# Sums of squares over feature blocks gathered on VectorE, and layer norms made in one pass, in a float32 two-block transformer kernel

## The reference

```python
def rms_norm(x, g):
    xf = x.astype(jnp.float32)
    y = xf * lax.rsqrt(jnp.mean(xf * xf, axis=-1, keepdims=True) + NORM_EPS)
    return (y * g.astype(jnp.float32)).astype(x.dtype)

def layer_norm(x, g, b):
    xf = x.astype(jnp.float32)
    mu = jnp.mean(xf, axis=-1, keepdims=True)
    var = jnp.mean(jnp.square(xf - mu), axis=-1, keepdims=True)
    return ((xf - mu) * lax.rsqrt(var + LN_EPS) * g + b).astype(x.dtype)

# first block
h = rms_norm(x, g_mix)                      # norm 1
...                                         # projections, sparse attention, conv, memory attention, gates
x = x + merged @ w_o
h = rms_norm(x, g_ffn)                      # norm 2
x = x + (silu(gate) * val) @ w_down         # gate, val: conv of h @ w_up; 2816 hidden features
x = rms_norm(x, g_final)                    # norm 3
# second block
...                                         # projections, stick-breaking attention, memory attention
x = layer_norm(ALPHA * x + y @ w_out, ...)  # norm 4
h = square(relu(x @ w_up))                  # 4096 hidden features
x = layer_norm(ALPHA * x + h @ w_down, ...) # norm 5, the output
```

## Time and profile before

| | us |
|---|---|
| time, median of 3 runs (3219.19 to 3224.37) | 3219.67 |
| time of the profiled execution | 3211.47 |
| its span in the trace | 3209.7 |
| TensorE busy (share of the span) | 3007.1 (94%) |
| VectorE busy | 1613.2 (50%) |
| GpSimd busy | 1149.3 (36%) |
| ScalarE busy | 754.9 (24%) |
| mean granted TensorE clock | 0.961 |

### The profile page before, as it was taken

The page is one execution under the profiler, slowest core; times in us unless marked ns, Lnnn a source line. Parts: engine busy times, 40 slices in busy tenths (PEclk is TensorE's granted clock), DMA queues, the critical chain, the costliest instruction groups (busy, mean ns, idle before and its releaser), DMA issues.

```text
span 3209.7 us, 35418 instructions
## 1 busy us (share of the span) xinstructions
PE 3007.1 (94%) x13506; PEld 2407.7 (75%) x13506; DVE 1613.2 (50%) x2187; ACT 754.9 (24%) x1320; POOL 1149.3 (36%) x649
## 2 busy tenths in 40 slices
PE   7887999998999999999999889999798999999997
PEld 5676778885776788888887568788575888888884
DVE  4476899885552423233232448888615322333333
ACT  3154010004511201101111256666403000000002
POOL 2230434441042343343344316555331433433430
PEclk9978999997999999999999899999899999999998
DMA  3100112221041111111111110000110111111111
GB/s 141 40 33 14 46 66 79 78 82 56 1 171 40 40 47 53 46 46 52 46 46 66 53 53 27 27 27 21 66 44 22 46 53 46 46 52 46 46 46 53
DMA packets 42300, 165.40 MB, mean 52 GB/s; under 512 B 4688, under 2 KB 5968, under 8 KB 40656
## 3 DMA queue, kind: packets, MB, share of 16 engines
q1 hardware_dynamic: 35568, 129.31, 12.0%
q10 hardware_dynamic: 6624, 34.61, 2.8%
HBM read 147.12 MB, written 16.78 MB: 51 GB/s over the span
## 4 chain that ended last, share of the span: by engine, by line
PE 81%; DVE 9%; issue 5%; ACT 2%; POOL 1%; DVEq 1%; DMA 1%; ACTq 0%; SPq 0%; POOLq 0%
PE dense L457 22%; PE dense L458 21%; PE dense L461 21%; PE side L497 2%; DVE stay L1603 2%; PE dense L789 2%; PE dense L790 2%; PE dense L791 2%; PE side L695 1%; PE dense L705 1%; PE side L827 1%; PE dense L622 1%; ACT T L972 1%; DVE a_lo L1281 1%; PE side L816 1%
## 5 line engine op out<-in xcount | busy, mean ns | idle before, releaser
L366 POOL TENSOR_TENSOR w_hi<-raw,zero 128x1024 fp32r<-128x1024 f32 x210 | 400.9, 1909 | 1624.3 <-PE dense L461 1512.6
L457 PE MATMUL dense<-a_hi,w_hi 128*128 128x512 f32 x2192 | 870.3, 397 | 42.5 <-DVE a_lo L1281 18.9
L458 PE MATMUL dense<-a_lo,w_hi 128*128 128x512 f32 x2192 | 861.2, 393 | 0.0
L461 PE MATMUL dense<-a_hi,w_lo 128*128 128x512 f32 x2192 | 680.7, 392 | 0.0
L457 PEld LDWEIGHTS dense<-a_hi,w_hi 128*128 128x128 f32 x2192 | 416.8, 190 | 143.5 <-issue 42.6
L368 POOL TENSOR_TENSOR w_lo<-raw,w_hi 128x1024 fp32r<-128x1024 f32 x210 | 514.1, 2448 | 16.5
L458 PEld LDWEIGHTS dense<-a_lo,w_hi 128*128 128x128 f32 x2192 | 416.9, 190 | 89.5 <-issue 3.6
L461 PEld LDWEIGHTS dense<-a_hi,w_lo 128*128 128x128 f32 x2192 | 415.8, 190 | 87.8
L457 PE MATMUL dense<-b_hi,w_hi 128*128 128x512 f32 x864 | 343.4, 397 | 4.0 <-DVE T L1517 2.5
L1502 DVE TENSOR_TENSOR x_res<-x_res,dense 128x1024 f32<-128x1024 f32 x112 | 136.7, 1221 | 403.8 <-PE dense L461 402.0
L458 PE MATMUL dense<-b_lo,w_hi 128*128 128x512 f32 x864 | 337.0, 390 | 0.0
(11 more groups left out here) (234 smaller groups left out, 3920.8 us busy)
## 6 DMA issues: line engine op xcount, KB each, us to landing
raw<-in_w_stream SPq DMA_DIRECT2D x231, 512.0 KB, 3.4
x_in<-in_x_t SPq DMA_DIRECT2D x4, 1024.0 KB, 8.0
spill_gate<-T ACTq DMA_DIRECT2D x8, 512.0 KB, 2.6
spill_part<-gates ACTq DMA_DIRECT2D x8, 512.0 KB, 2.7
back<-spill_gate ACTq DMA_DIRECT2D x8, 512.0 KB, 3.8
back<-spill_part ACTq DMA_DIRECT2D x8, 512.0 KB, 5.0
x_res<-in_x_t ACTq DMA_DIRECT2D x2, 2048.0 KB, 9.0
spill_x<-x_res ACTq DMA_DIRECT2D x1, 4096.0 KB, 14.1
```

Source lines behind the costliest of these rows:

```text
L366: pool.tensor_tensor(w_hi[:, r % 2, :], raw[:, r, :], zero[:, 0:1].broadcast_to([P, D]), ALU.add).then_inc(weights_rounded, 1)
L457: pe.matmul(o, w_hi[:, slot, w], hi[:, k, x], start=b == 0, stop=False)
L458: pe.matmul(o, w_hi[:, slot, w], lo[:, k, x], start=False, stop=False)
L461: last = pe.matmul(o, w_lo[:, slot, w], hi[:, k, x], start=False, stop=stop)
```

## The change

The change touches norms 1 to 5 and leaves the matrix products as they are.

- Norms 1 to 5: ACT writes the square of block 0 into `T[:, 3]`. VectorE adds the squares of blocks 1 to 6 into it, one instruction each (`add_square`), placed behind the residual addition of the block after. TensorE then takes ones products of two operands alone, `T[:, 3]` and the square of block 7, both after the last tile. ACT waits for VectorE's additions (`added`) where it waited for TensorE.
- Norms 4 and 5: VectorE also adds residual blocks 0 to 6 into `T[:, 2]` (`add_residual`, six instructions), and TensorE takes two ones products for the mean. ACT squares the blocks uncentred, as they come. The variance is the mean of squares less the square of the mean, formed on eight numbers for each partition after a second set of eight multiply-and-reduce instructions. The centring (L1639 before) comes after: three blocks while TensorE spreads the inverse deviation, the other five between the scale instructions.
- Norm 4: the multiplication by `ALPHA` (L1654) goes. The first group of the second feed-forward layer multiplies by it in its residual addition.
- The memory norm keeps its ones products.

```diff
+            def square_sums():
+                pe.wait_ge(added, norm_n["added"] + KB - 2)
+                sum_part(T[:, 3, :], S, 0, True, False)
+                pe.wait_ge(squares, norm_n["sq"] + KB)
+                sum_part(T[:, (KB - 1) % 2, :], S, 0, False, True).then_inc(sum_ready, 1)
+            def layer_norm(u):
+                pe.wait_ge(summed, norm_n["summed"] + KB - 2)
+                sum_part(T[:, 2, :], S, 1, True, False)
+                emptied(pe, u + KB - 1)
+                sum_part(x_res[:, KB - 1, :], S, 1, False, True).then_inc(mean_ready, 1)
+                square_sums()
+                spread(S, at=0)
...
-                    squares_part(n - 2)
-            rms(S, begin=KB - 2)
+            rms()
...
-                    residual_sum(n - 2, U_OUT2)
-            for k in (KB - 2, KB - 1):
-                residual_sum(k, U_OUT2)
-            rms(S)
+            layer_norm(U_OUT2)
...
-                    if k >= 2:
-                        act.wait_ge(squares_used, norm_n["used"] + k - 1)
-                    act.activation(T[:, k % 2, 0:width], src(k), ACT.Square).then_inc(squares, 1)
+                    if k >= 3:
+                        act.wait_ge(added, norm_n["added"] + k - 2)
+                    act.activation(T[:, k % 2 if k else 3, 0:width], src(k), ACT.Square).then_inc(squares, 1)
...
+            def add_square(k):
+                if 1 <= k < KB - 1:
+                    dve.wait_ge(squares, norm_n["sq"] + k + 1)
+                    if k > 1:
+                        dve.wait_ge(added, norm_n["added"] + k - 1)
+                    dve.tensor_tensor(T[:, 3, :], T[:, 3, :], T[:, k % 2, :], ALU.add).then_inc(added, 1)
+            def add_residual(n, u):
+                if 1 <= n < KB - 1:
+                    emptied(dve, u + n)
+                    emptied(dve, u + n - 1)
+                    if n > 1:
+                        dve.wait_ge(summed, norm_n["summed"] + n - 1)
+                    dve.tensor_tensor(T[:, 2, :], x_res[:, 0, :] if n == 1 else T[:, 2, :], x_res[:, n, :], ALU.add
+                                      ).then_inc(summed, 1)
+                add_square(n - 1)
+            def inverse_std(blocks, mean=False, at=1):
+                if mean:
+                    dve.wait_ge(mean_ready, norm_n["std"] - 4)
+                    for b in range(blocks):
+                        t = slice(b * P, b * P + P)
+                        dve.tensor_tensor_reduce(out=T[:, 2, t], in0=side[:, 1, t], in1=ident[:, :], scale=1.0, scalar=0.0,
+                                                 op0=ALU.mult, op1=ALU.add, accum_out=own_total[:, b:b + 1])
+                    dve.drain()
+                    dve.scalar_tensor_tensor(own_square[:, 0:blocks], own_total[:, 0:blocks], 1.0 / D, own_total[:, 0:blocks],
+                                             ALU.mult, ALU.mult)
...
+                if mean:
+                    dve.drain()
+                    dve.tensor_tensor(own_sum[:, 0:blocks], own_sum[:, 0:blocks], own_square[:, 0:blocks], ALU.subtract)
+                    dve.drain()
+                    last = dve.tensor_scalar(own_sum[:, 0:blocks], own_sum[:, 0:blocks], 0.0, None, ALU.max)
...
             dve.wait_ge(consts_in, CONSTS)
             for c in range(4):
                 dve.wait_ge(x_loaded[c], 16)
+            for k in range(KB):
+                add_square(k)
             inverse_std(TB)
...
             def layer_norm(gain, which):
-                for k in range(KB):
-                    dve.scalar_tensor_tensor(x_res[:, k, :], side[:, 1, :], -1.0 / D, x_res[:, k, :], ALU.mult, ALU.add
-                                             ).then_inc(centred, 1)
-                inverse_std(TB)
+                inverse_std(TB, mean=True)
+                for k in range(3):
+                    centre(k)
+                spread_in()
                 for k in range(KB + 1):
                     if k < KB:
                         if k >= 3:
                             dve.wait_ge(shifted, norm_n["shift"] + k - 2)
+                        dve.wait_ge(centred, norm_n["centred"] + k + 1)
+                        dve.scalar_tensor_tensor(third(k), x_res[:, k, :], par(gain, k), side[:, 0, :], ALU.mult, ALU.mult
                                                  ).then_inc(scaled, 1)
+                    if k + 3 < KB:
+                        centre(k + 3)
                     if k and which is not None:
                         m = k - 1
                         low((a_hi[:, m, :], a_lo[:, m, :]), m, x_res[:, m, :], which, m + 1)
-                        dve.drain()
-                        dve.tensor_scalar(x_res[:, m, :], x_res[:, m, :], ALPHA, None, ALU.mult)
```

More of the change, by code:

```diff
@@ L441, in _ @@
         def _(pe):
-            met_n, norm_n = [0], {"sq": 0, "mean": 0, "diag": 0}
+            met_n, norm_n = [0], {"sq": 0, "added": 0, "summed": 0, "diag": 0}
             def halves(psum, s, width=S):
@@ L491, in two_tiles, with sum_part, memory_squares, spread @@
                             last.then_inc(tile_done, 1)
-            def sum_part(k, src, width, at=0):
+            def sum_part(src, width, at, start, stop):
                 for c in range(0, width, 512):
                     e = min(width, c + 512)
-                    last = pe.matmul(side[:, at, c:e], ones[:, :], src[:, c:e], start=k == 0, stop=k == KB - 1,
-                                     skip_group_check=True)
-                return last
[L501 to L508, removed]
+                    last = pe.matmul(side[:, at, c:e], ones[:, :], src[:, c:e], start=start, stop=stop, skip_group_check=True)
+                return last
+            def memory_squares():
+                for k in range(KB):
+                    pe.wait_ge(squares, norm_n["sq"] + k + 1)
+                    last = sum_part(mem_squares[:, k, :], MEM, 0, k == 0, k == KB - 1)
+                last.then_inc(sum_ready, 1)
                 norm_n["sq"] += KB
+            def spread(width, at=1):
                 pe.wait_ge(diag_ready, norm_n["diag"] + 1)
@@ L722, in _, with group @@
                     tile(T_WO + n, T_WO + n)
-                    squares_part(n - 2)
-            rms(S, begin=KB - 2)
+            rms()
             def feed(t0, u0, ups, hidden, blocks, per, ready, n0):
-                def group(i, behind=None):
+                def group(i):
                     for c in range(ups):
@@ L763, in _ @@
                 tile(T_KV2 + n, U_KV2 + n, hi=m_hi, lo=m_lo, width=MEM, ready=parts["mem2"][1] if n == 0 else None)
-            feed(T_REST, U_REST, 2 * REST, hidden, REST, (0, 0), None, FULL * FG)(0, behind=squares_part)
-            rms(S, begin=KB - 2)
+            feed(T_REST, U_REST, 2 * REST, hidden, REST, (0, 0), None, FULL * FG)(0)
+            rms()
             two_tiles(T_MEM2, U_MEM2, parts["x2"][1])
@@ L885, in _ @@
         def _(act):
-            met_n, norm_n = [0], {"used": 0, "own": 0, "scaled": 0}
+            met_n, norm_n = [0], {"added": 0, "own": 0, "scaled": 0}
             def rms_squares(src, width, ready, dst=None):
@@ L1228, in _, with layer_norm @@
                 act.activation(a_hi[:, k, :], y2_f[:, k, :], ACT.Copy).then_inc(parts["y2"][0], 1)
[L1230 to L1237, removed]
+            def layer_norm(dst, which, shift, u):
+                rms_squares(lambda k: x_res[:, k, :], S, lambda k: emptied(act, u + k))
                 root(TB, EPS_LN)
                 round_scaled(dst, lambda k: T[:, (0, 1, 3)[k % 3], :], which, shift)
-            cen = [0]
-            layer_norm(a_hi, "x3", "ln1_b")
+            layer_norm(a_hi, "x3", "ln1_b", U_OUT2)
             def squared_relu(i):
@@ L1301, in _ @@
             dve.wait_ge(mem_loaded, 16)
+            norm_n["sq"] += KB
             inverse_std(MEM // P)
@@ L1492, in _, with down @@
                                   ).then_inc(parts["mem2"][1], 1)
-            def down(i, t0, u0, per, n0):
+            def down(i, t0, u0, per, n0, behind=None, scale=1.0):
                 for n in range(KB):
@@ L1669, in squared_relu @@
                                       ).then_inc(parts["hidden2"][1], 1)
-                down(i, T_FF2 + FG, U_FF2 + FG, FF2_TILES, 12 + FULL * KB // 2 + KB // 2)
-            repeat(dve, FF2_GROUPS, squared_relu)
+                down(i, T_FF2 + FG, U_FF2 + FG, FF2_TILES, 12 + FULL * KB // 2 + KB // 2, behind,
+                     ALPHA if isinstance(i, int) and i == 0 else 1.0)
+            repeat(dve, FF2_GROUPS - 1, squared_relu)
+            squared_relu(FF2_GROUPS - 1, behind=lambda n: add_residual(n, U_FF2 + (FF2_GROUPS - 1) * FF2_USES + FG))
+            add_square(KB - 1)
             layer_norm("ln2_g", None)
```

77 lines of the change are left out of this document (44 added, 33 removed).

## The result

The changed kernel takes 3180.61 us (median of 4 runs, 3176.68 to 3181.01), the kernel before 3220.63 us in the same comparison. The ratio is 0.9874, with a 95% interval of 0.9862 to 0.9885: 40.0 us or 1.2% less by the medians. The profiled execution after has a span of 3179.0 us; that of before had 3209.7, so the two traces differ by 30.7 only.

A forecast was written before the change was run, and what follows sets the result against it. TensorE was taken to bound the kernel (81% of the chain). Norms 1 to 5 sum as 9.9 - 6.1 - 3.7 - 20.5 - 20.3 = -40.7, so 3219.67 becomes 3179 us; range 3162 to 3196.

The forecast's parts named there:

- The ones products among the tiles cost their whole length: Norms 2 to 5: five products of 1.72 us leave the tiles ahead of each norm, -8.6 us each.
- The third rival: Products among the tiles are hidden anyway, because weights arrive no faster: -6.3 us in all, 3213; chance 0.04.
- An addition beside GpSimd waits for the running instruction: VectorE's SBUF additions: 1.2 us alone; beside GpSimd, the rest of its running instruction plus 1.1.
- The first rival: GpSimd does not hold VectorE's additions, which cost 1.2 to 1.3 us everywhere: -52.5 us, 3167; chance 0.14.
- the second rival: Gaps keep TensorE at half clock in norms 1 to 3 and norm 4's loop: -26.2 us in all, 3193; chance 0.15.
- Norm 1 becomes slower: Start of the kernel: additions wait for input and GpSimd, sum at 35.1 instead of 25.2, +9.9 us.
- The clock behind the gaps: Sums behind idle TensorE in norms 1 to 3: partly at half clock; norm 2 priced at 1.0 us, norm 3 at 1.5.
- the 4 us that I had named as a limit: Sign against the prediction: clock under 1.00 more than 4 us after dense work resumes.
- Norm 3: Short tiles: -8.6 us on TensorE, VectorE's last addition 5.2 behind it, slower products; -3.7 us in all.
- Norms 4 and 5: Layer norms: residual products leave the tiles, first scale 15.3 us after the last tile; -20.5 and -20.3 us.
- Slower by a lasting half clock: Half clock lasts through the second feed-forward after norm 4, deciding from 81 us on: +46 us, 3266; chance 0.03.

The follow-up runs named there:

- e2: The changed kernel with GpSimd's first two splits moved behind the six additions of norm 1; 3174.02 us.
- e1: The changed kernel with norm 1 alone put back: eight ones products on TensorE, no additions on VectorE; 3169.08 us, ratio 0.9847 to the kernel before.
- e5: The changed kernel with norms 4 and 5 put back (eight ones products for each sum, centring ahead of the squares); 3223.92 us, ratio 1.0009 to the kernel before.
- e4: The changed kernel with TensorE's gaps around the norms' sums and spreads filled with ones products that nobody reads; 3163.88 us.

## Why the prediction was right, step by step

The time was forecast as 3179, measured as 3180.61, and the sum of the forecast, -40.7, stands against -40.0. It holds by its steps too, with one of them mis-sized. That the two agree to 1.6 us is partly luck: the terms of the five norms add up to -37.7 in the traces, 3.0 short. With the long form of the sparse attention in both, the traces would differ by 38.9, the 37.7 and 1.2 from stages that the change doesn't touch.

- **The ones products among the tiles cost their whole length.** Right: from the first to the last residual addition norm 2 took 80.9 before and 72.0 after, norm 4 80.4 and 71.7, so 8.9 and 8.7 less, against the 8.6 forecast. The third rival, hidden products, is out.
- **An addition beside GpSimd waits for the running instruction.** Right, and shown: 14.83 for six with GpSimd, 7.87 without (e2), GpSimd's own instructions at 3.21 and 2.87. By the rule of the Trainium skill, "SBUF — State Buffer", section "Who interferes with whom", whoever issues first has the pair of ports for its whole instruction. The trace agrees: the 30 additions of squares took 1.22 to 3.42, median 1.97. The first rival, nearly free additions at 3167, is out (the prediction's second paragraph calls it the second rival by mistake).
- **Norm 1 becomes slower**, by 9.9. It was 11.8 in the trace. Of the 1.9 more, 0.7 are the later landing of the input in that execution (ACT starts at 7.91 and not at 7.21), and 1.1 the products, nearly all at half clock (6.32 for 5.2). e1 gives back 9.8 by its first dense product, 11.5 by the medians.
- **The clock behind the gaps** is the term that was mis-sized. I put the eight records of norm 1 at 5.2, of norm 2 at 4.4 and of norm 3 at 4.9, a value between full and half clock; they took 6.32, 6.49 and 6.08, close to all of them slow. In norm 2 it makes most of the difference between -6.1 and -3.5. I had bounded it from the gap of 2.40 us in the centred squares, which cost 1.7 in one norm of two, and in both in e5 (15.59 and 15.74). In this trace the gaps of 3.20 and 4.30 cost 3.1 and 2.6 of at most 3.4. Over the six traces that have both, the one of norm 3 cost that each time (records of 5.96 to 6.15 in sum), while the 3.20 of norm 2 cost from 0.3 to 3.1. So the bounds that I gave for norm 2, nothing to 3.4, hold, and no single value between them does. The second rival was thus half right: the short products of norms 1 to 3 ran mostly at half clock. Its other half, that the two tiles behind norm 4 stay slow, didn't happen: the part of norm 4 behind its last tile (E) ended 12.0 sooner, 11.9 forecast. Full clock did come back later, though: behind norms 1 to 4 the dense products ran at its pace (a start every 0.23 us, not 0.43) from 4.4, 4.7, 4.3 and 5.2 us after the first one, not 3.4, and over the 4 us that I had named as a limit. The limit was ill chosen. In the trace of before the four delays are 3.5, 4.0, 4.8 and 3.5, and I had read only the last. e4 shows what filling the gaps gives back of all this: 16.7 us.
- **Norm 3.** -3.7 and -3.7. Weights in time, VectorE 4.3 behind TensorE (5.2 forecast), and slower products in return (6.08 for 4.9): two errors of about one us that cancel.
- **Norms 4 and 5.** From the last tile to the first scale instruction 15.5 and 15.0 us, 15.3 forecast. The last shift came 16.1 behind the first scale instruction, 16.7 forecast: a step of VectorE there lasts 2.33, not 2.4. e5 confirms their weight: 43.3 for 40.8.
- **Slower by a lasting half clock.** It lasted 4.3 to 5.2 us behind norms 1 to 4, far from the 81 from which it would have decided.

What luck there was lies in two places: about 4 us that the clock took beyond the forecast are partly made up for by a norm 5 that gained 1.3 more and by VectorE's lesser delay in norm 3 (0.9), and there is the stage of sparse attention. The forecast took the difference between profiled execution and median as the same for both kernels. It was 8 us for the one and 0 for the other, by the two forms of that stage, and since I applied the sum to the median of before, it did no harm.

## What to carry to other kernels

A reduction that moves from the busiest engine to an idle one isn't free there: count which other engine's instructions it has to take turns with at that moment, and what it waits for that the old place did not. What paid here were the layer norms, which became one pass: they gave 42 us, while the three RMS norms, where only the sums moved, gained 7 in two places and lost 12 in the third. Of the 42 some 17 are ones products of the residual that left the tiles (an estimate, twice the 8.7 of norm 4), which is the move, and 25 the shorter stretch behind them. No run separates the two: a kernel with one pass whose sums all stay on TensorE wasn't tried. And in a relay between engines, it can pay to keep TensorE busy across short gaps, behind which its few small products mostly cost nearly double here; fillers gave 17 us for nothing but instructions.

## What the runs showed of the hardware that I had not expected

- Fillers on TensorE that nobody reads shorten a kernel that TensorE bounds: 16.7 us, for 96 added records, 41 us of work at 0.43 each.
- The same gap ahead of the same instructions can cost nearly nothing or nearly the whole of half clock: 3.70, 5.40 or 6.45 to 6.58 us for eight records behind 3.20 us, in kernels that don't differ at this place.
- One stage of small products with a granted clock of 0.82 to 0.87 takes either 148 to 150 or 156 to 158 us, in executions of the same instructions. The medians of a kernel with both forms move by 8 us with the share of each, five runs or fewer do not settle that share, and a profiled execution can be of the rarer form. In the two traces set side by side the difference lies in 26 us of the stage, where full clock returned sooner in one. What decides between the two wasn't tried.
